# A two-block transformer kernel on one core: memory norm inside the value loop, fp32 memory units, two norms in one pass

## The reference

```python
# end of block 1
x = x + gt2 * peer_ffn(h2, ...)          # mixture of 16384 experts, dense here: u1, v1
x = rmsnorm(x, final_g)
# start of block 2
h  = rmsnorm_2(x, norm1_g[l])            # a norm of a normed x
z  = h @ w_in[l]                         # fq, fk, fv, ff, sq, sk, sv, mq, gl
mn = rmsnorm_2(mem, mem_norm_g[l])       # 256 memory rows, an input
mk, mv = split(mn @ w_mem_kv[l])         # 1024 x 1024: 8 units below
```

## Time and profile before

| | |
|---|---|
| median of 3 runs | 2428.82 us (2426.08 to 2429.02) |
| the profiled execution | 2426.62 us |
| its span, first to last instruction | 2424.9 us |
| PE busy | 2293.4 us (95%) |
| DVE, ACT, POOL busy | 1686.9, 1273.3, 187.9 us |
| mean granted TensorE clock | 0.986 |

### The profile page before, as it was taken

One profiled execution on the slowest core, in us unless ns is written; L12 is line 12 of the kernel. 1 busy time (PEld: TensorE's weight loads), 2 busy tenths in 40 slices (PEclk: granted clock), 3 DMA queues, 4 the chain that ended last, 5 costly groups with the idle time before them and its releaser, 6 DMA issues.

```text
span 2424.9 us, 47283 instructions
## 1 busy us (share of the span) xinstructions
PE 2293.4 (95%) x15320; PEld 2091.8 (86%) x15320; DVE 1686.9 (70%) x3481; ACT 1273.3 (53%) x2778; POOL 187.9 (8%) x253
## 2 busy tenths in 40 slices
PE   5998999999997899999899999999999987999998
PEld 4996899999997788888788888999999976888887
DVE  7675666888877866666645557458888869666665
ACT  3453345555557755555546653445555568555554
POOL 0000000000005800000000000000000039000000
PEclk8998999999999999999999999999999999999999
DMA  9751354555551055555334324445555520555554
GB/s 371 282 191 35 106 207 139 182 182 182 182 189 53 33 192 192 194 193 191 130 112 140 123 96 145 146 142 183 182 182 182 183 94 0 169 195 190 192 195 149
DMA packets 106080, 389.73 MB, mean 161 GB/s; under 512 B 12032, under 2 KB 12160, under 8 KB 105232
## 3 DMA queue, kind: packets, MB, share of 16 engines
q1 hardware_dynamic: 104688, 381.73, 46.2%
q10 hardware_dynamic: 992, 4.88, 0.5%
q0 software_dynamic: 320, 2.13, 0.2%
HBM read 387.64 MB, written 1.05 MB: 160 GB/s over the span
## 4 chain that ended last, share of the span: by engine, by line
PE 82%; POOL 7%; DVE 6%; ACT 3%; DMA 1%; issue 1%; SPq 0%; POOLq 0%; DVEq 0%; ACTq 0%
PE ps L592 19%; PE ps L559 16%; PE ps L554 16%; PE ps L556 16%; PE ps L596 10%; POOL scores L444 7%; DMA big<-ada_in 1%; DVE lo L1256 1%; DVE act_lo L1333 1%; DVE big L1340 1%; PE ps L706 1%; PE ps L673 1%; DVE act_hi L1332 1%; ACT big L1020 1%; PE ps L694 0%
## 5 line engine op out<-in xcount | busy, mean ns | idle before, releaser
L944 ACT ACTIVATE hi<-raw 128x512 fp32r<-128x512 f32 x1356 | 776.7, 620 | 80.9 <-PE ps L559 78.5
L1256 DVE TENSOR_TENSOR lo<-raw,hi 128x512 fp32r<-128x512 f32 x844 | 547.0, 689 | 169.1 <-ACT hi L944 168.2
L554 PE MATMUL ps<-act_hi,hi 128*128 128x256 f32 x3376 | 552.0, 286 | 13.4 <-ACT hi L944 6.2
L559 PE MATMUL ps<-act_hi,lo 128*128 128x256 f32 x3376 | 546.3, 285 | 11.4 <-DVE lo L1256 11.4
L556 PE MATMUL ps<-act_lo,hi 128*128 128x256 f32 x3376 | 544.9, 284 | 0.0
L554 PEld LDWEIGHTS ps<-act_hi,hi 128*128 128x128 f32 x3376 | 467.8, 193 | 27.0 <-issue 13.8
L559 PEld LDWEIGHTS ps<-act_hi,lo 128*128 128x128 f32 x3376 | 468.4, 193 | 12.8 <-DVE lo L1256 12.8
L556 PEld LDWEIGHTS ps<-act_lo,hi 128*128 128x128 f32 x3376 | 467.6, 193 | 0.0
L1531 DVE TENSOR_TENSOR lo<-raw,hi 128x512 fp32r<-128x512 f32 x512 | 329.8, 688 | 131.6 <-ACT hi L944 124.3
L979 ACT ACTIVATE big<-ps 128x256 f32 (+1 forms) x346 | 132.7, 383 | 526.5 <-PE ps L559 526.5
L592 PE MATMUL ps<-hi,act_hi 128*128 128x512 f32 x1024 | 399.3, 390 | 0.0
(11 more groups left out here) (190 smaller groups left out, 1568.2 us busy)
## 6 DMA issues: line engine op xcount, KB each, us to landing
raw<-u SPq DMA_DIRECT2D x256, 512.0 KB, 4.1
raw<-v SPq DMA_DIRECT2D x256, 512.0 KB, 3.4
raw<-front SPq DMA_DIRECT2D x166, 512.0 KB, 3.5
big<-ada_in SPq DMA_DIRECT2D x48, 512.0 KB, 5.5
big<-biasA_in ACTq DMA_DIRECT2D x1, 2048.0 KB, 10.0
xT<-xT_in ACTq DMA_DIRECT2D x1, 1024.0 KB, 10.3
big<-keys_in ACTq DMA_DIRECT2D x1, 1024.0 KB, 13.3
scores<-memT_in POOLq DMA_DIRECT2D x1, 1024.0 KB, 5.2
```

Source lines behind the costliest of these rows:

```text
L554: pe.matmul(out_ap, hi_l(k), hi_r(k), start=(first and k == 0), stop=False, skip_group_check=True)
L559: mm = pe.matmul(out_ap, lo_l(k), hi_r(k), start=False, stop=(last and k == n - 1), skip_group_check=True)
L944: act.activation(hi[:, s, :, :], raw[:, rs, 4 * h:4 * h + 4, :], ACT.Copy).then_inc(hi_done, 1)
L1256: dve.tensor_tensor(lo[:, s, :, :], raw[:, rs, 4 * h:4 * h + 4, :], hi[:, s, :, :].bitcast(F32), ALU.subtract).then_inc(lo_done, 1)
```

## The change

It has three parts.

1. **The memory's norm moves into `v1`.** The first 7 turns (28 units) of `v1`, and of `v2`, are written out in place of one. In those of `v1`, behind the work for a unit: ACT squares one tile of `memT` after each of units 4 to 11; DVE adds the eight squares up in a tree of three adds after units 13 to 15; PE makes one fp32 matmul with `ones` after unit 15; ACT makes Ln and Exp after unit 16; DVE scales one tile of `memT` in place after each of units 18 to 25. The function table is loaded ahead of `v1`.
2. **The memory units are plain fp32.** `mk` and `mv` (now of kind "F") are no longer rounded and split: PE multiplies `raw` by `memT` directly, 8 matmuls of 128x256 a unit. A slot of `raw` is free once PE is done with it (`mem_used`).
3. **The final norm and `norm1_2` are one pass.** With r1 the final norm's rsqrt, the second one is rsqrt(r1*r1*mean((x*final_g)^2) + eps). ACT makes both sets of squares from `xT`, DVE adds each up in a tree, PE makes one matmul for each behind unit 2 of `mk`, and `tmp` is scaled by both at once and split for the queries. The `keep_busy` calls of this stage are gone.

Two small arrays move into `cols`, and DVE makes the product of the two gains at the start. The core of the diff:

```diff
-    Run("mk", "T", 4), Run("mv", "T", 4), Run("sk", "T", 1), Run("sv", "T", 1),
+    Run("mk", "F", 4), Run("mv", "F", 4), Run("sk", "T", 1), Run("sv", "T", 1),
+MEM_SQUARE_AT, MEM_TREE_AT, MEM_SUM_AT, MEM_RSTD_AT, MEM_APPLY_AT = 4, 13, 15, 16, 18
+V_PEEL = 7
...
+            def mem_run(name, after=None):
+                r = RUNS[name]
+                pe.wait_ge(mem_ready, KT)
+                for u in range(r.units):
+                    n, o = r.unit0 + u, r.out0 + u
+                    pe.wait_ge(raw_in[n % RAW], 16 * (n // RAW + 1))
+                    pe.wait_ge(taken, o - 1)
+                    for k in range(KT):
+                        mm = pe.matmul(po[o % 2], raw[:, n % RAW, k, :], memT[:, k, :], start=(k == 0), stop=(k == KT - 1))
+                    mm.then_inc(mem_used, 1)
+                    if after is not None:
+                        after(u)
...
+                    if b == 1 and u == MEM_SUM_AT:
+                        pe.wait_ge(mem_tree, 3)
+                        pe.matmul(bw[1][:, 0:T], ones[:, :], mem_sq[:, 0, :], start=True, stop=True).then_inc(mem_sum, 1)
...
-            norm_sum("mem")
-            norm_sum("final")
-            keep_busy(9)
-            run("mk", "mem")
-            run("mv")
+            def after_key(u):
+                if u == 2:
+                    for i in range(2):
+                        pe.wait_ge(fin_tree, 3 * i + 3)
+                        pe.matmul(bw[i][:, 0:T], ones[:, :], fin_sq[i][:, 0, :], start=True, stop=True).then_inc(fin_sum, 1)
+            mem_run("mk", after_key)
+            mem_run("mv")
             to_tokens("mv")
-            keep_busy(6)
-            norm_sum("norm1_2")
-            keep_busy(17)
...
# ACT
+                if b == 1:
+                    act.preload_act_table_set(LN_EXP)
...
+                    if 0 <= kt < KT:
+                        act.activation(mem_sq[:, kt, :], memT[:, kt, :], ACT.Square).then_inc(mem_sq_s, 1)
+                    if u == MEM_RSTD_AT:
+                        act.wait_ge(mem_sum, 1)
+                        link(act.activation(mem_r[:, 0, :], bw[1][:, 0:T], ACT.Ln, bias=eps[:, :], scale=1.0 / D))
+                        act.activation(mem_r[:, 1, :], mem_r[:, 0, :], ACT.Exp, scale=-0.5).then_inc(mem_rstd, 1)
...
+            for kt in range(KT):
+                act.wait_ge(x_tile, kt + 1)
+                act.activation(fin_sq[0][:, kt, :], xT[:, kt, :], ACT.Square).then_inc(fin_sq_s, 1)
+                act.activation(fin_sq[1][:, kt, :], xT[:, kt, :], ACT.Square, scale=col("final_g", kt)).then_inc(fin_sq_s, 1)
+            for u in range(3):
+                mem_out("mk", mkT, u)
+            act.wait_ge(fin_sum, 1)
+            link(act.activation(fin_r[:, 0, :], bw[0][:, 0:T], ACT.Ln, bias=eps[:, :], scale=1.0 / D))
+            act.activation(fin_r[:, 1, :], fin_r[:, 0, :], ACT.Exp, scale=-1.0).then_inc(fin_r1, 1)
+            act.activation(fin_r[:, 2, :], fin_r[:, 0, :], ACT.Exp, scale=-0.5).then_inc(fin_r1, 1)
+            act.wait_ge(fin_q, 1)
+            link(act.activation(fin_r[:, 3, :], fin_r[:, 3, :], ACT.Ln, bias=eps[:, :], scale=1.0 / D))
+            act.activation(fin_r[:, 4, :], fin_r[:, 3, :], ACT.Exp, scale=-0.5).then_inc(fin_r2, 1)
...
# DVE
+            for i in range(2):
+                dve.wait_ge(fin_sq_s, 2 * KT - 1 + i)
+                for level in range(3):
+                    square_tree(fin_sq[i], level, fin_tree, 3 * i + level + 1)
+            dve.wait_ge(fin_sum, 2)
+            dve.wait_ge(fin_r1, 1)
+            dve.tensor_tensor(fin_r[:, 3, :], bw[1][:, 0:T], fin_r[:, 1, :], ALU.mult).then_inc(fin_q, 1)
+            dve.wait_ge(fin_r1, 2)
+            dve.wait_ge(fin_r2, 1)
+            link(dve.tensor_tensor(fin_r[:, 5, :], fin_r[:, 2, :], fin_r[:, 4, :], ALU.mult))
+            for c in (0, 4):
+                for kt in range(c, c + 4):
+                    ins = dve.scalar_tensor_tensor(out=tmp[:, kt, :], in0=xT[:, kt, :], scalar=final_gain[:, kt:kt + 1],
+                                                   in1=fin_r[:, 5, :], op0=ALU.mult, op1=ALU.mult)
+                    ins.then_inc(n_scaled, 1)
+                dve.wait_ge(n_scaled, 16 + c + 4)
+                split_part(c, tmp[:, c:c + 4, :])
```

More of the change, by code:

```diff
@@ L102, in place_runs @@
         r.unit0, r.half0, r.out0, r.block = unit, half, out, block
-        r.outs = {"T": r.units, "K": 2 * r.units, "U": r.units, "O": 0}[r.kind]
+        r.outs = {"T": r.units, "F": r.units, "K": 2 * r.units, "U": r.units, "O": 0}[r.kind]
         unit += r.units
-        half += 2 * r.units
+        half += 0 if r.kind == "F" else 2 * r.units
         out += r.outs
         RUNS[r.name] = r
-    stored = [r for r in RUN_LIST if r.kind in "TK" and r.name not in STORED_LATER]
+    stored = [r for r in RUN_LIST if r.kind in "TKF" and r.name not in STORED_LATER]
     for name, behind in reversed(STORED_LATER.items()):
@@ L313, in two_blocks_kernel @@
         act_ready = sem("activations_split")
+        mem_sq_s, mem_tree, mem_sum, mem_rstd = (sem(f"mem_{n}") for n in ("squares", "square_tree", "sum", "rstd"))
+        mem_ready, mem_used = sem("mem_normalised"), sem("mem_units_used")
+        fin_sq_s, fin_tree, fin_sum = sem("final_squares"), sem("final_square_trees"), sem("final_sums")
+        fin_r1, fin_q, fin_r2 = sem("final_rstd"), sem("second_square_sum"), sem("second_rstd")
         x_ready = sem("residual_ready")
@@ L371, in _, with free @@
         def _(sp):
-            def free(n):
+            def free(n, block):
                 if is_static(n) and n < RAW:
                     return
-                sp.wait_ge(lo_done, (n - RAW + 1) * 2)
+                first, count = RUNS["mk"].unit0, RUNS["mk"].units + RUNS["mv"].units
+                if is_static(n) and first <= n - RAW < first + count:
+                    sp.wait_ge(mem_used, n - RAW - first + 1)
+                elif block == 2 and not (is_static(n) and n - RAW < first):
+                    sp.wait_ge(lo_done, (n - RAW + 1 - count) * 2)
+                else:
+                    sp.wait_ge(lo_done, (n - RAW + 1) * 2)
             def load_ada(tile):
@@ L623, in body @@
                             half(r, g, j, h)
-                        if after is not None:
+                        if after is not None and is_static(g):
                             after(g * GROUP + j)
@@ L629, in run @@
                 else:
-                    groups(pe, r, body, peel=1 if after is None else r.units // GROUP)
+                    groups(pe, r, body, peel=peel or (1 if after is None else r.units // GROUP))
             def to_tokens(name):
@@ L1172, in _, with mem_out @@
             experts(1)
-            act.wait_ge(mem_in_s, 16)
-            norm_squares("mem", memT)
-            norm_squares("final", xT, (x_tile, 0))
-            norm_rstd("mem")
-            norm_rstd("final")
-            last_out = run("mk", to(mkT), defer=True)
-            run("mv", to(values["mv"][0]), lead=last_out)
+            def mem_out(name, dst, u):
+                act.wait_ge(mem_used, RUNS[name].unit0 - RUNS["mk"].unit0 + u + 1)
+                act.activation(dst[:, u, :], po[(RUNS[name].out0 + u) % 2], ACT.Copy).then_inc(taken, 1)
+            for kt in range(KT):
[11 more added lines that the diff above has]
+            act.activation(fin_r[:, 4, :], fin_r[:, 3, :], ACT.Exp, scale=-0.5).then_inc(fin_r2, 1)
+            mem_out("mk", mkT, 3)
+            for u in range(4):
+                mem_out("mv", values["mv"][0], u)
             copy_tokens("mv")
-            act.wait_ge(x_ready, 3)
-            act.wait_ge(act_ready, 2 * EV["mem"] + 2)
-            norm_squares("norm1_2", xT)
-            norm_rstd("norm1_2")
             last_out = run("sk", to(skT), defer=True)
@@ L1509, in experts, with after_value @@
                 r = RUNS[f"v{b}"]
+                def after_value(u):
+                    if u == MEM_TREE_AT:
+                        dve.wait_ge(mem_sq_s, KT)
+                    if 0 <= u - MEM_TREE_AT < 3:
+                        square_tree(mem_sq, u - MEM_TREE_AT, mem_tree, u - MEM_TREE_AT + 1)
+                    kt = u - MEM_APPLY_AT
+                    if kt == 0:
+                        dve.wait_ge(mem_rstd, 1)
+                    if 0 <= kt < KT:
+                        dve.scalar_tensor_tensor(out=memT[:, kt, :], in0=memT[:, kt, :], scalar=col("mem_g", kt),
+                                                 in1=mem_r[:, 1, :], op0=ALU.mult, op1=ALU.mult).then_inc(mem_ready, 1)
                 def body_v(g):
@@ L1524, in experts, with square_tree @@
                     dve.tensor_copy(vout[:, 0, 512 * half:512 * half + 512], vsum[0][half]).then_inc(v_taken[0], 1)
+            def square_tree(squares, level, ready, count):
+                n = KT >> (level + 1)
+                dve.tensor_tensor(squares[:, 0:n, :], squares[:, 0:n, :], squares[:, n:2 * n, :], ALU.add)\
+                    .then_inc(ready, 1)
```

(1 more changed line is left out.)

51 lines of the change are left out of this document (30 added, 21 removed).

## The result

| | before | changed |
|---|---|---|
| median, runs of one chip | 2427.45 us (2425.91 to 2429.02, 4 runs) | 2401.64 us (2399.42 to 2402.36, 4 runs) |
| the profiled execution | 2426.62 | 2402.24 |
| its span | 2424.9 | 2400.5 |
| mean granted clock in it | 0.986 | 0.983 |

The changed kernel takes 0.9893 of the time before, with a 95% interval of 0.988 to 0.9905: 26.0 us less by the ratio. The forecast was 2401.0 within 2397 to 2407.

The account below looks back on a forecast made before the run. PE was taken to bound the kernel. Its stage between `v1` and `sk` falls from 63.58 to 36.5, 27.1 less; minus 0.44 in `v1` gives 26.7, so 2399.9 or 2402.1 by starting point; 2401 taken, range 2397 to 2407.

Parts of the forecast that it names:

- turning of the sums: PE's first work behind `v1`, turning its sums: taken as unchanged, 1.97 us.
- eight memory units: `mk` and `mv` on PE in plain fp32: 3.56 us a unit, 28.5 in all, 5.4 more than in three passes.
- eviction of `mv`: Stretch behind the last matmuls of `mv`, before `mv` is turned: 0.64 us.
- the stage: PE's time from the start of turning `v1`'s sums to the first matmul of `sk`: 36.5 us against 63.58.
- PE alone sets the stage: Between `v1` and `sk`, PE's own work in its order was summed to 36.5 us, with the norms hidden.
- The price of an fp32 matmul: Memory units: 0.445 us per plain fp32 matmul of 128x256, from the eight of `norm_sum`; new weights add nothing.
- The rival with an fp32 matmul at four times an fp32r one: Memory units: 0.48 us a matmul instead of 0.445, 2.2 us more, 2403; chance 0.04.
- The cover of the merged norm: Splits ready at 1215.8, PE asks at the forget gate about 1225.2: 9.4 us spare; late-norm rival 2403, chance 0.05.
- The work in `v1` is hidden: ACT's and DVE's memory-norm work fits their idles in `v1`; only PE's 0.44 us counts; rival unhidden, 2410, chance 0.06.
- The tightest place: In `v1`, ACT's wait for the memory norm's sum with unit 17 queued behind it: holds with 0.6 us to spare.
- The loads of the queries: Rival: `raw` slots freed only by PE delay four units from `sk` on, 6 us, 2407, chance 0.03; first load 14 ahead.
- The clock: 1.00 granted throughout; rival: half clock from first memory unit to forget gate, 33.9 us paid twice, 2435, chance 0.02.

Follow-up runs that it names:

- three-pass version: Changed kernel with `mk` and `mv` rounded and split again for three fp32r passes, `memT` split as before: 2407.05 us, ratio 0.992 to the kernel before.
- two norms: Changed kernel with the final norm and `norm1_2` done one after the other again: 2399.00 us, ratio 0.9888 to the kernel before.
- a chain 5.8 later: Changed kernel with three unread DVE products of `memT` put ahead of the merged norm's combined scale: 2398.72 us in one run.

## Why the prediction was right

The steps in their order, with what was measured in the changed kernel:

| step of the sum | predicted | measured |
|---|---|---|
| turning of the sums | 1.97 | 1.81 |
| eight memory units | 28.5 | 27.6 |
| two norm sums | 0.89 | 0.86 |
| eviction of `mv` | 0.64 | 0.64 |
| turning of `mv` | 0.92 | 1.02 |
| forget gate | 3.55 | 3.55 |
| the stage | 36.5 | 35.5 |
| `v1` | +0.44 | +0.45 |

- **PE alone sets the stage: right.** The terms add up to the stage with nothing left over (the eviction is read as the stretch from the last matmul of `mv`, at the pace of 0.216 a record, to the turning of `mv`). That PE's order is the bound holds only for the changed kernel; in the three-pass version and in the kernel before, splits and norms are.
- **The price of an fp32 matmul: right in kind, mis-sized by 3%.** The step took 0.445 from eight matmuls at the head of the stage. The memory units run at 10.36 / 24 = 0.432 each, 0.9 us less for all eight, and this is nearly the whole miss of the stage; the rest is the turning of the sums, for which the length of the row (1.97) was taken and not the 1.8 to the next start. The earlier trace rows had the better price: nine `keep_busy` matmuls have 4.05 in their row and six have 2.76, so three more cost 1.29, 0.43 each. New weights for each matmul cost nothing. The rival with an fp32 matmul at four times an fp32r one, 0.48, fell: 0.432 was measured. The Trainium skill ("FP8 and Floating Point Precision", TensorE Precision Notes) says that true fp32 takes four passes through the array. No run here counts the passes; four of them in 0.432 would be 0.108 each, an estimate, less than the 0.12 of an fp32r matmul by which the rival priced them.
- **The cover of the merged norm: right, 8.9 for 9.4.** The half us that is missing is not the chain's: its last split ends 23.1 behind the start of the turning, where 23.5 was forecast, but PE asks at 32.0 and not at 32.9, since the memory units are faster. The squares were mis-sized: a pair takes 0.70 to 0.72 and not 0.65, because the one whose scale is read from memory takes 0.40, 5.7 in all for 5.2. It cost nothing, but it was near: the trees are ready at 1202.23 + 4.86 = 1207.1 and PE comes to the sums at 1207.79, 0.7 later, where 1.5 was forecast. The margin ahead of the forget gate was not needed: with 2.2 of cover (two norms) and with a chain 5.8 later the stage was 35.51.
- **The work in `v1` is hidden: right.** PE's only addition shows. The tightest place, unit 17, held:

```profile
889.56 0.59 PE L788 MATMUL ps<-scores,ones 128*128 128x256 f32 x2
...
892.76 0.39 PE L611 MATMUL ps<-hi,act_hi 128*128 128x512 f32 x1
```

```profile
891.46 0.43 DVE L1594 TENSOR_TENSOR act_lo<-big,act_hi 128x256 fp32r<-128x256 f32 x1 [2.15 <-ACT act_hi L1158]
```

  The activation's `lo` is there at 891.89 and PE's unit 17 starts at 892.76: 0.9 to spare, where 0.6 was forecast. How far the idles reach is measured by the squares: two more a unit are free, five more cost 8.1.
- **The loads of the queries: right.** PE shows no wait for `raw` in the stage or behind it. The load of `sk` was issued at 1215.76, 15.4 ahead of its first matmul; the 14 of the prediction should have been 15.8 by its own terms.
- **The clock: right.** 1.00 throughout. Where a part is undone, waits of PE return and stretches at half clock with them, and both are in the worth of the part: 2.4 of the 12.15 of part 1, and some 5.0 of the 8.98 of part 2. One reading is not borne out: the prediction puts the fall of the clock to a long idle alone, and in the three-pass version it fell behind idles of 0.78, 0.49 and 1.26. The new stage has only 0.79 and, 30 us later, 0.47.
- **The total is right partly by luck of the execution.** The stage gained 1.0 more than forecast. The profiled execution of the change came to 2402.24 all the same, because `v1` started 2.83 late, in a stretch that differs by up to 5 us between executions and that no step of the sum priced. The range had 3 us for it. Apart from that stretch the gain is 27.2 to 27.6, where the sum had 26.7.

Undone one at a time, part 1 is worth 12.15 us of the stage, part 2 8.98 and part 3 nothing. They don't add up to 28.07, since each was measured with the other two in place; what part 3 is worth where `memT`'s norm is still ahead of it was not tried. The three loads of the function table that the stage had before, 1.28 each, are gone in every version of the changed kernel, and no run prices them.

## What to carry to other kernels

Price a stage by the one engine that should bound it after the change, row by row, and then ask of every other chain only when it is ready and when it is asked for; what is ready 2 us early is worth as much as what is ready 9 us early. An operation that is dearer on the bounding engine can still pay if it takes preparation away from the engines that it waits for: here 4.6 us more of PE's work saved 9. Where waits can't be removed, matmuls that nobody reads are worth their queue slots if PE's own work is the bound behind the wait (5.1 us for 23 of them here), and nothing if what follows waits for another engine anyway (the nine ahead of `mk`). Where the waits go, such matmuls go with them.
